# Spreading the running sums of a state-space scan over partitions by 32-row groups of ones

## The chip, the cores and the metric

One NeuronCore of a Trainium2 chip runs the whole kernel in one launch. The metric is the device time of an execution in microseconds (us). Two layers run in one loop on the chip, so each stage shows twice in a trace.

## The reference

The kernel is one inference step of a hybrid trunk: 128 context tokens and 256 latent tokens, width 1024, two layers. Each layer mixes tokens in three branches (latent attention, gated linear attention, and the state-space branch C), adds them through sigmoid gates, and then runs a mixture of experts. Only branch C is touched. Per head it does

```
acum   = cumsum(dt * A)                          # along the tokens of a chunk
Lm     = exp(acum[i] - acum[j])  for j <= i, else 0
y_diag = sum_j (C_i . B_j) * Lm[i, j] * dt_j * x_j
y_off  = (C_i . state) * exp(acum_i)
state  = exp(acum_last) * state + sum_j exp(acum_last - acum_j) dt_j x_j B_j
```

with 16 heads of 64 columns, two groups of B and C with 128 states each, and two directions. The matrix acum[i] - acum[j] is what the change is about: one factor of it, acum[i], has to lie along the free axis and be the same on all partitions j.

## The kernel before

Tokens come in three tiles of 128: tile 0 is the context, tiles 1 and 2 the latent tokens. The scan of branch C is one block of code with a stream of instructions for each engine (TensorE, VectorE, ScalarE, GpSimd, and SyncE for DMA), ordered by semaphores alone. It goes over six steps, `SCAN = ((0, 0), (1, 0), (0, 1), (1, 2), (0, 2), (1, 1))`, each a pair (direction d, tile t). The order within an engine is the order of the code.

TensorE, per step: `sc` (L1350), four matmuls of 16 columns that give the sums of 16 heads by token; `cb` (L1354), the products of B and C of two groups; `ai` (L1361), 16 matmuls, one for each head, of a column of `dta` broadcast to 128 by 128 as the stationary operand with the triangular matrix `rel(d)` as the moving one, four heads to a PSUM bank; `yo` (L1372, only t > 0), the old state times C; then a tile of the sigmoid gate of this branch, 16 records of L293, which has nothing to do with the scan and is put there as other work; `ds` (L1379, not in steps 4 and 5), what a step adds to the state; `yd` (L1387), 16 matmuls of 64 columns; and after tile 0 the transposes `so` (L325) of the state for the output. An fp32 matmul shows as two records in the trace.

VectorE, per step: `cb` times a mask (L1451); for each quarter q of the heads a subtraction from PSUM (L1457), a minimum with zero (L1461), and, one quarter late, a product with the masked `cb` (L1465); then the sums of y (L1472 and L1476 for `yo`, L1479 for `yd`), the state (L1486 for tile 0, else L1491 and L1493), and a one-column copy (L1496) that carries the semaphore `state_ready`. ScalarE copies and exponentiates `sc` into `ex2` (L1404, L1406) and exponentiates each quarter (L1410). GpSimd makes x times dt (L1436, L1439). Before the steps VectorE copies four transposed states (L1447).

The eight PSUM banks are handed out in turn: `claim` waits until the last user of the next bank was read, `makes` and `made` are the semaphore of a filled bank, `reads` and `read` that of a bank that was read. What stands behind a waiting claim on TensorE waits too.

After the scan TensorE runs the last two gate tiles (32 records of L293), while VectorE and ScalarE normalise y; the next block transposes y (L325).

Of the kernel before, what the change touches and what calls it, by code (L numbers as in the profile page):

```python
# [20 lines left out]
ALU = mybir.AluOpType  # L21
# [3 lines left out]
P = 128  # L25
# [62 lines left out]
GRP = 32  # L88
# [3 lines left out]
def trunk_kernel(nc, x, cond, consts, iota, vecs, rows, w_small, w_gate_low, router_w, cache_ckv, cache_krope,  # L92
                 state_gla, state_ssd, w_ada, w_in, a_wq, a_wkv, a_wo, b_wo, c_wo, w_out, e_w1, e_w3, e_w2,
                 y, new_ckv, new_krope, new_gla, new_ssd):
    with ExitStack() as ctx:
        def sb(name, shape):
            return ctx.enter_context(nc.sbuf_tensor(name, shape, F32))
# [15 lines left out]
        pick_row = sb("pick_row", [P, 2])  # L113
        mod = sb("mod", [P, 6, KD, 2])
# [14 lines left out]
            "xbc_ready", "ssd_state_in", "diff_ready", "decayed_ready", "mask_ready", "xw_ready",  # L129
# [21 lines left out]
        def counts(name):  # L151

            count[name] = count.get(name, 0) + 1
            return sem[name], 1
# [330 lines left out]
        with nc.Block() as block:  # L485
# [15 lines left out]
            @block.vector  # L501
            def _(dve):
                dve.memset(lowT[2 * RANK:2 * RANK + 1, :], 1.0).then_inc(*counts("dve_step"))
                dve.wait_ge(*counted("dve_step"))
                dve.memset(scond[:, :, :], 0.0).then_inc(*counts("cond_clear"))
                dve.wait_ge(*counted("cond_clear"))
                dve.wait_ge(sem["xin"], 64)
                ids = ident.rearrange("p (g r) -> p g r", r=GRP)
                dve.tensor_reduce(pick_row[:, 0:1], ids[:, :, 0], AX_X, ALU.add).then_inc(*counts("dve_step"))
                dve.tensor_reduce(pick_row[:, 1:2], ids[:, :, 1], AX_X, ALU.add).then_inc(*counts("dve_step"))  # L510
                dve.wait_ge(*counted("dve_step"))
                features_dve(dve, "x", xT)
# [55 lines left out]
        with nc.Fori(0, DEPTH) as l:  # L568
# [660 lines left out]

            gT_c = [carve(9728 + T * k, T) for k in range(3)] + [carve(3072 + T * k, T) for k in range(KD - 3)]  # L1230
# [106 lines left out]
            with nc.Block() as block:  # L1337
                @block.tensor
                def _(pe):
                    gate_pe(pe, W_GC, "gc", 0)  # L1340
                    pe.wait_ge(*following(pe, "ssd_state_in", 32))
                    for d in range(2):
                        for q in range(2):
                            transposed(pe, ("si", d, q), [ssd_in[:, d, 4 * q + i, :] for i in range(4)])
                    for s, (d, t) in enumerate(SCAN):
# [10 lines left out]
                        ins.then_inc(*makes(("cb", s)))  # L1356
                        for q in range(4):
                            out = claim(pe, ("ai", s, q))
                            for i in range(4):
                                h = H_C * d + 4 * q + i  # L1360
                                ins = pe.matmul(out[:, P * i:P * i + P], dta[:, t, h:h + 1].broadcast_to([P, P]), rel(d),  # L1361
                                                start=True, stop=True)
                            ins.then_inc(*makes(("ai", s, q)))
# [10 lines left out]
                        if s + 1 < len(SCAN):  # L1374
                            gate_pe(pe, W_GC, "gc", s + 1)
# [66 lines left out]
                def _(dve):  # L1442
                    dve.wait_ge(*following(dve, "yoff_ready"))
                    for d in range(2):
                        for q in range(2):
                            dve.wait_ge(*made(("si", d, q)))
                            dve.tensor_copy(ssd_s[:, d, 512 * q:512 * q + 512], bank(("si", d, q))).then_inc(*reads(("si", d, q)))  # L1447
                            dve.wait_ge(*read(("si", d, q)))
                    for s, (d, t) in enumerate(SCAN):
                        dve.wait_ge(*made(("cb", s)))  # L1450
# [3 lines left out]
                        for q in range(5):  # L1454
# [7 lines left out]
                            if q:  # L1462
# [4 lines left out]
                                dve.wait_ge(*counted("mask_ready"))  # L1467
                        for g in range(G_C):
# [698 lines left out]
```

## Time and profile before

| | us |
|---|---|
| median of 3 runs (2783.02 to 2785.2) | 2784.48 |
| profiled execution | 2785.75 |
| its span, first to last instruction | 2783.9 |
| TensorE busy | 2454.4 |
| VectorE busy | 893.8 |
| mean granted TensorE clock | 0.927 |
| scan of branch C in layer 1 (first `sc` to the last gate tiles) | 772.8 to 883.5 |
| same in layer 2 | from 2151.8 |

In the trace PE is TensorE's matmul, PEld its load of a stationary operand, DVE is VectorE, ACT ScalarE, POOL GpSimd, SP SyncE. L1361 is line 1361 of the kernel. PEclk is the granted share of TensorE's clock: 1.00 is 2.4 GHz, 0.50 is 1.2 GHz. A row of a timeline merges instructions of one kind that follow each other closely; behind its count, in brackets, is the idle time of the engine before it and what ended it. Busy times of matmuls are modelled ends, so the start of the next line is the better mark.

### The profile page before, as it was taken

What the parts mean: (1) busy time and instruction counts of PE and PEld (TensorE: products, weight loads), DVE (VectorE), ACT (ScalarE), POOL (GpSimd) and SP (SyncE); (2) the same over time, 40 slices, a digit from 0 to 9 for tenths busy, and PEclk for the clock granted to TensorE, in tenths of its full rate; (3) what the DMA queues carried; (4) which work ended last, traced back from release to release, by engine and by line L of the source; (5) the groups of instructions that cost most, each with busy time, mean ns of one, the idle gap of its engine ahead of it and who ended that gap; (6) DMA issues with size and microseconds to landing.
All of it is one profiled execution on the core that took longest, in us unless ns stands there. A gap on an engine that the chain in (4) does not pass through costs nothing. (4 is left out here: it accounts for less than half of the span.)

```text
span 2783.9 us, 39618 instructions
## 1 busy us (share of the span) xinstructions
PE 2454.4 (88%) x16902; PEld 1508.4 (54%) x16902; DVE 893.8 (32%) x1492; ACT 510.1 (18%) x906; POOL 106.0 (4%) x74
## 2 busy tenths in 40 slices
PE   6999999889899969999479999997898999599893
PEld 3546654554576545555245476555545765455552
DVE  2255312431558130000113562224315661300002
ACT  1133202210223021010021241022102220201000
POOL 0000000000021000000000000001001110000000
PEclk8999999899989979999789999898999899699996
DMA  6321132114314277999353201411243222799972
GB/s 241 106 93 61 54 140 93 46 61 151 125 32 146 91 297 272 376 373 345 115 184 112 93 31 62 165 61 46 71 159 117 89 78 91 298 346 379 375 272 80
DMA packets 162338, 440.60 MB, mean 158 GB/s; under 512 B 10150, under 2 KB 50086, under 8 KB 153448
## 3 DMA queue, kind: packets, MB, share of 16 engines
q1 hardware_dynamic: 144360, 412.75, 40.6%
q10 hardware_dynamic: 14336, 12.59, 1.5%
q0 software_dynamic: 3456, 12.58, 1.2%
q8 instruction: 140, 2.29, 0.3%
q14 instruction: 46, 0.38, 0.0%
HBM read 400.38 MB, written 37.52 MB: 157 GB/s over the span
## 5 line engine op out<-in xcount | busy, mean ns | idle before, releaser
L293 PE MATMUL ps<-space 128*128 128x384 f32 (+3 forms) x1696 | 475.5, 433 | 14.9 <-DVE space L469 8.5
L293 PE MATMUL ps<-hT,space 128*128 128x384 f32 x1344 | 461.3, 504 | 27.3 <-ACT hT L407 12.1
L293 PEld LDWEIGHTS ps<-space 128*128 128x128 f32 x1696 | 300.1, 194 | 187.7 <-issue 48.4
L293 PEld LDWEIGHTS ps<-hT,space 128*128 128x128 f32 x1344 | 262.0, 197 | 213.4 <-issue 41.4
L1673 PE MATMUL ps<-space 128*32 128x256 f32 x6144 | 343.7, 384 | 1.7 <-ACT space L1783 1.5
L293 PE MATMUL ps<-space,hT 128*128 128x512 f32 x768 | 336.7, 599 | 3.8 <-PEq L1191 3.8
L1673 PEld LDWEIGHTS ps<-space 128*32 128x32 f32 x6144 | 201.9, 111 | 133.8 <-issue 12.6
L293 PEld LDWEIGHTS ps<-space,hT 128*128 128x128 f32 x768 | 146.9, 192 | 192.0 <-issue 191.4
L1694 PE MATMUL ps<-space 128*32 128x256 f32 x3072 | 184.2, 398 | 1.5 <-DVE space L1915 1.5
L325 PE MATMUL ps<-cst,space 128*128 128x128 f32 x492 | 84.6, 324 | 90.5 <-DVE space L1927 29.8
L1694 PEld LDWEIGHTS ps<-space 128*32 128x32 f32 x3072 | 100.9, 115 | 74.2 <-issue 15.8
L325 PEld LDWEIGHTS ps<-cst,space 128*128 128x128 f32 x492 | 67.3, 167 | 119.7 <-DVE space L1927 32.4
L1910 DVE TENSOR_TENSOR space<-ps,space 128x384 f32<-128x384 f32 x32 | 17.8, 558 | 344.3 <-ACT space L1792 344.3
L381 DVE COPY space<-ps 128x512 f32<-128x512 f32 x24 | 16.6, 691 | 247.6 <-PE ps L366 247.5
L1656 PE MATMUL ps<-cst,space 96*128 96x96 f32 x256 | 31.8, 274 | 72.5 <-DMA space<-h_rows 72.3
L366 PE MATMUL ps<-space,scond 128*32 128x512 f32 x384 | 49.2, 637 | 42.6 <-issue 30.7
L293 PE MATMUL ps<-mT,space 128*128 128x384 f32 x256 | 83.1, 487 | 3.0 <-DVE space L1550 3.0
L1792 ACT ACTIVATE space<-ps 128x384 f32<-128x384 f32 x32 | 15.7, 490 | 331.3 <-PE ps L1673 331.3
L1915 DVE COPY space<-ps 128x384 f32<-128x384 f32 x32 | 17.8, 558 | 173.0 <-PE ps L325 173.0
L1656 PEld LDWEIGHTS ps<-cst,space 96*128 96x128 f32 x256 | 25.2, 154 | 86.4 <-DMA space<-h_rows 47.7
L293 PEld LDWEIGHTS ps<-mT,space 128*128 128x128 f32 x256 | 48.5, 190 | 37.6 <-DVE space L1550 4.2
L837 PE MATMUL ps<-space 96*128 96x384 f32 (+1 forms) x192 | 68.5, 442 | 0.1
(255 smaller groups left out, 2262.7 us busy)
## 6 DMA issues: line engine op xcount, KB each, us to landing
space<-in_e_w SPq DMA_DIRECT2D x96, 2048.0 KB, 15.2
space<-in_w_in SPq DMA_DIRECT2D x36, 2048.0 KB, 8.5
space<-in_w_ada SPq DMA_DIRECT2D x24, 2048.0 KB, 8.2
h_rows<-space SPq DMA_DIRECT2D x2, 6144.0 KB, 25.7
space<-h_rows SPq DMA_DIRECT2D x32, 384.0 KB, 17.9
y_rows<-mT ACTq DMA_DIRECT2D x128, 96.0 KB, 10.4
space<-in_a_wo SPq DMA_DIRECT2D x4, 2048.0 KB, 11.4
space<-in_b_wo SPq DMA_DIRECT2D x4, 2048.0 KB, 8.2
```

Of the source, the lines that this page charges most:

```text
L293: ins = pe.matmul(out, a, b, start=(i == 0), stop=(i == len(pairs) - 1))
L325: ins = pe.transpose(out[0:s.shape[1], i * P:i * P + P], s, ident)
L366: ins = pe.matmul(out[GRP * g:GRP * g + GRP, :], scond[:, k, :], w[:, k, :], start=(i == 0), stop=(i == KD // NGRP - 1))
L381: dve.tensor_copy(rows, bank(("mr", n))).then_inc(*reads(("mr", n)))
L837: pe.matmul(out[:, 0:P * (k1 - k0)], head_qT[0:QK, h % 2, tok(t)], head_kT[0:QK, h % 2, P * k0:P * k1], start=True, stop=True).then_inc(*m ...
L1656: ins = pe.transpose(out[:, SLOTS * i:SLOTS * i + SLOTS], tok_in[0:SLOTS, e % 2, P * k:P * k + P], ident[0:SLOTS, 0:SLOTS])
L1673: ins = pe.matmul(ps[TILE * c:TILE * c + TILE, B_UP + i // 2, 2 * P * (i % 2):2 * P * (i % 2) + 2 * P], hc[:, k, TILE * i:TILE * i + TILE] ...
L1694: ins = pe.matmul(ps[TILE * c:TILE * c + TILE, B_Y + i // 2, QD * (i % 2):QD * (i % 2) + QD], hidden[:, k, TILE * i:TILE * i + TILE], w2[: ...
L1792: act.activation(silc, up[:, :, up_first(e), :], ACT.Silu).then_inc(*counts("gated_ready"))
L1910: dve.tensor_tensor(gated, up[:, :, 1 - up_first(e), :], silc, ALU.mult).then_inc(*reads(("up", e)))
L1915: dve.tensor_copy(hidden.rearrange("p c (i s) -> p c i s", s=TILE), src).then_inc(*reads(("hid", e)))
```

## The change

The 16 matmuls of a step that broadcast one head each (L1361) go. In their place VectorE deals the 16 columns of `dta` into a matrix `dealt` of 128 columns that is zero elsewhere: head 4g + r goes to column 32g + r (`deal`). One matmul (`ar`) of this matrix with `rel(d)` gives the running sums of the 16 heads, head 4g + r on partition 32g + r. VectorE multiplies them by `pick_four`, a 128 by 4 matrix with ones where the partition is r modulo 32, into `block_rows`, 128 by 512, in which the partition 32g + r holds its head in columns 128r to 128r + 127 and zeros elsewhere (`blocks`), and a one-column copy carries the semaphore `block_ready`. Four matmuls then take 32 partitions each: ones (32 rows by 128 columns) as the stationary operand, 32 rows of `block_rows` with 512 columns as the moving one, each into a bank of its own, so that the sum over the 32 partitions spreads four heads over all 128 partitions, in the form that L1457 read before.

The deal and the block of a step are made in the step before it: `deal(s + 1)` at the start of step s, `ar` of s + 1 ahead of the gate tile, `blocks(s + 1)` behind the last product (L1465). Those of step 0 stand ahead of the steps, its block behind the four copies of L1447. The four banks of `ai` are now claimed one after the other before the first of the four matmuls, and `ar` takes one bank more in the round. `dealt` and `block_rows` lie in `wsm`, whose weights are used up by then.

```diff
--- before.py
+++ after.py
@@ -111,6 +111,7 @@
         condT = sb("condT", [P, KD, 2])
         scond = sb("scond", [P, KD, GRP])
         pick_row = sb("pick_row", [P, 2])
+        pick_four = sb("pick_four", [P, 4])
         mod = sb("mod", [P, 6, KD, 2])
         amp = sb("amp", [P, 2, KD, 2])
         dtraw = sb("dtraw", [P, NT, 32])
@@ -126,7 +127,7 @@
             "h_ready", "cqn_ready", "ckvn_ready", "sq_ready", "summed", "stat_ready", "head_root", "rotary_in",
             "nmax_ready", "abs_ready", "soft_ready", "logdecay_ready", "clamped_ready", "decay_ready",
             "qk_ready", "gla_state_in", "scaled_state", "state_ready", "o_ready", "conv_ready",
-            "xbc_ready", "ssd_state_in", "diff_ready", "decayed_ready", "mask_ready", "xw_ready",
+            "xbc_ready", "ssd_state_in", "diff_ready", "dealt_ready", "block_ready", "decayed_ready", "mask_ready", "xw_ready",
             "yoff_ready", "y_ready", "merged_ready", "chosen_ready", "zeros_ready", "zeroed", "rows_ready", "y_summed", "gated_ready", "y_scaled", "hidden_ready", "moe_ready", "stored",
             "act_step", "dve_step", "pool_step")
         sem = {n: ctx.enter_context(nc.semaphore(n)) for n in names}
@@ -508,6 +509,9 @@
                 ids = ident.rearrange("p (g r) -> p g r", r=GRP)
                 dve.tensor_reduce(pick_row[:, 0:1], ids[:, :, 0], AX_X, ALU.add).then_inc(*counts("dve_step"))
                 dve.tensor_reduce(pick_row[:, 1:2], ids[:, :, 1], AX_X, ALU.add).then_inc(*counts("dve_step"))
+                dve.wait_ge(*counted("dve_step"))
+                dve.tensor_reduce(pick_four[:, :], ident.rearrange("p (g r) -> p r g", r=GRP)[:, 0:4, :], AX_X, ALU.add
+                                  ).then_inc(*counts("dve_step"))
                 dve.wait_ge(*counted("dve_step"))
                 features_dve(dve, "x", xT)
 
@@ -1227,6 +1231,9 @@
             ssd_out = (carve(8192, KD, P), carve(25200, KD, P))
             ssd_tmp = carve(9216, 512)
 
+            w_flat = wsm[:, :, :].rearrange("p k n -> p (k n)")
+            block_rows = w_flat[:, 0:512]
+            dealt = w_flat[:, 512:768].rearrange("p (b n) -> p b n", b=2)
             gT_c = [carve(9728 + T * k, T) for k in range(3)] + [carve(3072 + T * k, T) for k in range(KD - 3)]
             mod_rows_c = carve(19344, 3, 512)
             zeros = carve(26256, QD)
@@ -1342,6 +1349,13 @@
                     for d in range(2):
                         for q in range(2):
                             transposed(pe, ("si", d, q), [ssd_in[:, d, 4 * q + i, :] for i in range(4)])
+
+                    def cumulative_rows(s):
+                        pe.wait_ge(*following(pe, "dealt_ready"))
+                        pe.matmul(claim(pe, ("ar", s))[:, 0:P], dealt[:, s % 2, :], rel(SCAN[s][0]), start=True, stop=True
+                                  ).then_inc(*makes(("ar", s)))
+
+                    cumulative_rows(0)
                     for s, (d, t) in enumerate(SCAN):
                         col = slice(OUT_COL[t], OUT_COL[t] + P)
                         a = dta[:, t, H_C * d:H_C * d + H_C]
@@ -1354,13 +1368,12 @@
                             ins = pe.matmul(out[:, P * g:P * g + P], xbc[:, 8 + g, col], xbc[:, 10 + g, col],
                                             start=True, stop=True)
                         ins.then_inc(*makes(("cb", s)))
+                        pe.wait_ge(*following(pe, "block_ready"))
                         for q in range(4):
-                            out = claim(pe, ("ai", s, q))
-                            for i in range(4):
-                                h = H_C * d + 4 * q + i
-                                ins = pe.matmul(out[:, P * i:P * i + P], dta[:, t, h:h + 1].broadcast_to([P, P]), rel(d),
-                                                start=True, stop=True)
-                            ins.then_inc(*makes(("ai", s, q)))
+                            claim(pe, ("ai", s, q))
+                        for q in range(4):
+                            pe.matmul(bank(("ai", s, q)), ones[GRP * q:GRP * q + GRP, :], block_rows[GRP * q:GRP * q + GRP, :],
+                                      start=True, stop=True).then_inc(*makes(("ai", s, q)))
                         if t:
                             for g in range(G_C):
                                 if s in FIRST:
@@ -1372,6 +1385,7 @@
                                 pe.matmul(claim(pe, ("yo", s, g)), xbc[:, 10 + g, col],
                                           ssd_s[:, d, 512 * g:512 * g + 512], start=True, stop=True).then_inc(*makes(("yo", s, g)))
                         if s + 1 < len(SCAN):
+                            cumulative_rows(s + 1)
                             gate_pe(pe, W_GC, "gc", s + 1)
                         pe.wait_ge(*following(pe, "xw_ready"))
                         if s not in LAST:
@@ -1440,13 +1454,34 @@
 
                 @block.vector
                 def _(dve):
+                    dve.memset(dealt, 0.0).then_inc(*counts("dve_step"))
+                    dve.wait_ge(*counted("dve_step"))
+                    dve.tensor_copy(dealt[:, 0, :].rearrange("p (g r) -> p g r", r=GRP)[:, :, 0:4],
+                                    dta[:, 0, 0:H_C].rearrange("p (g r) -> p g r", r=4)).then_inc(*counts("dealt_ready"))
                     dve.wait_ge(*following(dve, "yoff_ready"))
                     for d in range(2):
                         for q in range(2):
                             dve.wait_ge(*made(("si", d, q)))
                             dve.tensor_copy(ssd_s[:, d, 512 * q:512 * q + 512], bank(("si", d, q))).then_inc(*reads(("si", d, q)))
                             dve.wait_ge(*read(("si", d, q)))
+
+                    def deal(s):
+                        d, t = SCAN[s]
+                        out = dealt[:, s % 2, :].rearrange("p (g r) -> p g r", r=GRP)[:, :, 0:4]
+                        dve.tensor_copy(out, dta[:, t, H_C * d:H_C * d + H_C].rearrange("p (g r) -> p g r", r=4)
+                                        ).then_inc(*counts("dealt_ready"))
+
+                    def blocks(s):
+                        dve.wait_ge(*made(("ar", s)))
+                        dve.tensor_tensor(block_rows.rearrange("p (r n) -> p r n", r=4), each(bank(("ar", s))[:, 0:P], 4),
+                                          over(pick_four[:, :], P), ALU.mult).then_inc(*reads(("ar", s)))
+                        dve.wait_ge(*read(("ar", s)))
+                        dve.tensor_copy(stat_c[:, 0:1], cst[:, 0:1]).then_inc(*counts("block_ready"))
+
+                    blocks(0)
                     for s, (d, t) in enumerate(SCAN):
+                        if s + 1 < len(SCAN):
+                            deal(s + 1)
                         dve.wait_ge(*made(("cb", s)))
                         dve.tensor_tensor(cbm, quad(bank(("cb", s))[:, 0:G_C * P]), each(cum(d), G_C), ALU.mult).then_inc(*reads(("cb", s)))
                         dve.wait_ge(*read(("cb", s)))
@@ -1465,6 +1500,8 @@
                                 dve.tensor_tensor(decayed[:, 4 * r:4 * r + 4, :], quad(diff[:, r % 2, :]),
                                                   each(cbm[:, r // 2, :], 4), ALU.mult).then_inc(*counts("mask_ready"))
                                 dve.wait_ge(*counted("mask_ready"))
+                        if s + 1 < len(SCAN):
+                            blocks(s + 1)
                         for g in range(G_C):
                             out = y_c[:, t, 512 * g:512 * g + 512]
                             if t:
```

## Rows read from the trace of the kernel before

**Rows 1.** The page's table of engines: busy us, share of the span, instructions.
```profile
PE 2454.4 (88%) x16902; PEld 1508.4 (54%) x16902; DVE 893.8 (32%) x1492; ACT 510.1 (18%) x906; POOL 106.0 (4%) x74
```

**Rows 2.** Groups by line: engine, operation, tiles, shape, count | busy us, mean ns | idle before.
```profile
L1361 PE MATMUL ps<-cst,space 128*128 128x128 f32 x384 | 52.3, 300 | 0.3
...
L1457 DVE TENSOR_TENSOR space<-ps,space 128x512 f32<-128x512 f32 x48 | 33.1, 689 | 8.5 <-PE ps L1361 6.1 <-ACT space L1406 1.1
```

**Rows 3.** Stretches by step: us, busy of PE, PEld, DVE, ACT, POOL, PEclk, DMA share, GB/s.
```profile
772.80:792.40 19.60, 17.25 (x107) 14.06 (x106) 14.41 (x21) 5.97 (x9) 3.86 (x2) 0.92 0.00 1
792.40:815.40 23.00, 20.65 (x106) 17.46 (x106) 12.04 (x20) 5.97 (x9) 3.86 (x2) 0.80 0.00 0
815.40:834.60 19.20, 19.20 (x101) 15.17 (x101) 11.93 (x20) 5.97 (x9) 3.86 (x2) 0.88 0.20 65
834.60:852.00 17.40, 17.33 (x102) 13.10 (x102) 15.81 (x25) 5.97 (x9) 4.30 (x2) 1.00 1.06 368
852.00:867.70 15.70, 15.63 (x98) 12.37 (x98) 14.95 (x23) 5.97 (x9) 4.29 (x2) 1.00 0.37 119
867.70:883.50 15.80, 13.04 (x82) 11.76 (x82) 14.97 (x22) 4.20 (x7) 3.86 (x2) 0.83 0.00 1
```

**Rows 4.** Stretches at the lower clock: three of the first layer, one of the second.
```profile
789.40:799.50 10.10, 8.84 (x42) 8.87 (x43) 4.93 (x9) 2.31 (x4) 3.42 (x2) 0.50 0.01 2
813.30:820.00 6.70, 6.36 (x30) 6.39 (x31) 2.06 (x5) 1.68 (x3) 1.01 (x1) 0.50 0.01 2
878.10:888.30 10.20, 10.20 (x35) 8.08 (x35) 9.42 (x12) 2.93 (x5) 0.00 (x0) 0.50 0.01 2
...
2168.40:2178.50 10.10, 8.86 (x42) 8.89 (x43) 4.93 (x9) 2.31 (x4) 3.44 (x2) 0.50 0.01 2
```

**Rows 5.** Timeline, steps 0 and 1: start, length, engine, line, tiles, count [idle before, releaser].
```profile
771.80 2.87 DVE L1447 COPY space<-ps 128x512 f32<-128x512 f32 x4 [9.57 <-PE ps L325]
...
774.18 3.74 PE L1361 MATMUL ps<-cst,space 128*128 128x128 f32 x32
...
777.75 5.33 PE L293 MATMUL ps<-hT,space 128*128 128x384 f32 x16
...
782.91 1.88 PE L1379 MATMUL ps<-space 128*128 128x512 f32 x4
...
784.63 3.68 PE L1387 MATMUL ps<-space 128*128 128x64 f32 x32
...
786.63 0.69 DVE L1479 TENSOR_TENSOR space<-ps,space 128x512 f32<-128x512 f32 x1 [1.69 <-PE ps L1387]
...
790.66 1.94 PE L325 MATMUL ps<-cst,space 128*128 128x128 f32 x8 [2.35 <-DVE space L1486]
...
794.95 5.27 PE L1361 MATMUL ps<-cst,space 128*128 128x128 f32 x26
...
800.73 5.33 PE L293 MATMUL ps<-hT,space 128*128 128x384 f32 x16
```

**Rows 6.** Timeline, end of the scan.
```profile
877.36 6.41 PE L1387 MATMUL ps<-space 128*128 128x64 f32 x32 [2.76 <-issue]
...
883.56 12.90 PE L293 MATMUL ps<-hT,space 128*128 128x384 f32 x32
```

**Rows 7.** Timeline of TensorE: 32-column groups of L366 between full matmuls.
```profile
703.71 1.92 PE L366 MATMUL ps<-space,scond 128*32 128x512 f32 x16
705.56 10.91 PE L293 MATMUL ps<-hT,space 128*128 128x384 f32 x33
```

**Rows 8.** Timeline, start of step 3.
```profile
834.64 1.02 PE L1350 MATMUL ps<-space,cst 128*128 128x16 f32 x8
...
836.03 4.07 PE L1361 MATMUL ps<-cst,space 128*128 128x128 f32 x32
...
838.93 0.15 DVE L1496 COPY space<-cst 128x1 f32<-128x1 f32 x1
838.95 0.97 PEld L1361 LDWEIGHTS ps<-cst,space 128*128 128x128 f32 x8 [0.26 <-DVE space L1493]
```

## The prediction

> **What bounds the kernel now.** I read the busy table first. TensorE is busy for 88% of the span and VectorE for 32% [rows 1], so on average TensorE sets the time; but the change touches one stage, so that stage has to be read by itself. The groups by line say what leaves: the 384 head records of L1361 are 52.3 us of both layers [rows 2], 4.4 us a step for 12 steps. That is an upper bound of the gain, worth its face only where TensorE's end is what the step waits for. The stretches by step (first layer) show that this changes inside the stage: steps 0 to 2 last 19.6, 23.0 and 19.2 us with VectorE busy 14.4, 12.0 and 11.9; steps 3 to 5 last 17.4, 15.7 and 15.8 with VectorE busy 15.8, 15.0 and 15.0 [rows 3]. In the first three TensorE, partly at its lower clock, is the limit; in the last three the two engines are nearly level, with VectorE short of idle time.
>
> The same rows and the stretches by clock show the second thing: the granted clock is half (1.2 instead of 2.4 GHz) for some 10 us from 789.4, 6.8 us from 813.3 and 10 us from 878.1, and the second layer repeats the first of them [rows 4]. Each begins around a pause of TensorE: 2.35 us idle at 790.66 behind the 64-column matmuls of L1387 and ahead of the 16-column ones of L1350, and 2.76 us at 877.36 [rows 5, 6]. At half clock the 16 gate matmuls (5.33 us at full) take about twice that.
>
> **The matmuls removed and added.** Removed are 32 records of 128 columns a step. At full clock they run from 774.18 to the gate's start at 777.75, 3.6 us [rows 5]; in steps 1 and 2 they are stretched by the low clock. Added are 8 records with 32 rows and 512 columns a step (four matmuls, each with two records as every fp32 one here), and two of 128 columns (0.22) for the running sums. No row shows 32-row groups. Upper bound: one after another, as the 512-column records of L1379, 4 in 1.72 us (782.91 to 784.63 [rows 5]), so 3.4 us. Lower bound: side by side, as the 32-column groups of L366, whose 16 records of 512 columns take 1.85 us from the first start to the next line's [rows 7], so 0.9 us for 8. I take 0.9, the nearest row, being also a quarter of the array per matmul; each writes a bank of its own.
>
> Going into a group and out again costs something: L366's 16 records would be four times 0.43, 1.71 us, and 1.85 passed [rows 7], so 0.1 to 0.2 us a step. The Trainium skill, TensorEngine Tiling (Array Packing), section Key Properties, says that a change of tiling mode (not of the tile alone) drains TensorE. Were only a change of tile at issue the term would be zero; by the rule each of 12 steps pays twice, some 2 us in all, and the 1.85 us of L366 agrees with it.
>
> **Work added to VectorE.** A step gains the deal (a copy of 16 columns: between L1496's 0.15 and L1457's 0.69 us; I take 0.17, as it is small like the first), the block product (512 columns out of PSUM with a broadcast operand, the form of L1457, 0.69) and the marker copy (0.15), with 0.03 between them: 1.1 us [rows 2, 8]. Ahead of the scan a memset and a deal lie in VectorE's 9.57 us of idling before L1447 [rows 5]; the reduction for pick_four lies before the layers, below 0.2 us. In steps 0 to 2 the 1.1 us lies in idle time (1.69 us before the first L1479 of step 0; by the busy times 5.2 us of step 0, 11.0 of step 1 and 7.3 of step 2 [rows 3]). In steps 3 to 5 that cover is gone: there it costs up to its own length in each step that has it (3 and 4).
>
> **Two new waits.** (a) TensorE now waits for block_ready ahead of the four matmuls. In step 0 the product stands behind four copies that end at 774.67 [rows 5]: 774.67 + 0.9 + a semaphore's 0.06 is 775.65 against a start at 774.18. Then 0.95 of matmuls, 0.22 and 0.2 of switching put the gate at 777.0 instead of 777.75: only 0.7 us early. From step 1 on the block is made a step ahead. (b) All four banks are claimed before the first matmul. Banks go round by eight, and by my count of the claims the third and fourth ones of steps 3 and 4 are those that the state update of the step before still has to read. Before, 24 of the 32 head records of such a step ran ahead of it and only the last 8 waited (838.95, released by L1493 [rows 8]). Now all of them wait, and behind them in TensorE's queue the yo matmuls, the next sums, the gate, ds and yd. TensorE is left with sc and cb (834.64 to 836.03, 1.4 us) for the 4.3 us from there to that release: it idles 2.9 us where it idled 0.26.
>
> **The sum, one layer.** Steps 0 to 2, if the clock keeps its pattern: 0.7 in step 0; in step 1 the heads shrink from 5.8 us (794.95 to 800.73 [rows 5]) to 1.9 at half clock, but the gate, 4 us earlier, runs its first five matmuls at half, which leaves 2.1; step 2 the same way, until VectorE binds, 0.8: together -3.6. If the clock stays low as long as TensorE has this much less to do, the earlier gate is simply slower: 0. I take the middle, -1.8. Step 3: from release to release TensorE needs 0.95 + 0.2 + 1.72 (yo) + 0.22 + 5.2 (gate) + 1.72 (ds) + 1.8 (first half of yd) = 11.8, then VectorE 8 operations of 0.725 = 5.8: 17.6 against 17.4 now, +0.2 to +0.4. To this comes the clock. An idle time of 2.9 us, with L1387 before it and the few-column sc beside it, is longer than the one of 2.35 that ended in half clock in both layers [rows 4, 5]; so I expect one more slow stretch in step 3 and one in step 4. The shorter kind (6.8 us) takes 3.4 us, the longer 5.1: step 3 +3.7. Step 4, without ds: release to end of yd 0.95 + 0.2 + 1.72 + 0.22 + 5.2 + 3.6 = 11.9, 15.3 with 3.4 lost, against 11.4 now; some of it lies beside VectorE's own +1.6 (1.1 of work and 0.5 of waiting for the first group): between +1.6 at full clock and +3.9, taken +3.0. Step 5 has VectorE's work unchanged and a longer TensorE pause ahead of yd, and behind the scan 32 gate matmuls of 12.90 us that half clock already stretches [rows 6]: 0 to +3.4, taken +1.0. Sum: -1.8 + 3.7 + 3.0 + 1.0 = +5.9 a layer, +11.8 for two.
>
> The profiled execution took 2785.75 us (span 2783.9 and 1.85 around it), 1.3 above the median of the runs, 2784.48. With the sum it would be 2797.6; set against the median, **2796**.
>
> **Rivals.** Full clock in the wait (not slower): the idle time of steps 3 and 4 stays below what lowers the clock. For it: 2.76 and 2.35 are not far off, and in steps 3 and 4 of now the clock is 1.00 [rows 3]; against it, both shorter pauses did lower it. Then -3.6 + 0.3 + 1.6 = -1.7 a layer, -3.4 in all, 2781. It decides wherever the granted clock of the stretch from the end of step 2 to the end of step 4 is above 0.95.
>
> The pauses at the ends of steps 0 and 1 stop lowering the clock as well, since they fall earlier: 5.1 and 3.4 us are to be had there, less what VectorE then limits, some 1.5: -7 a layer, 2770. Against it, the pauses themselves (VectorE's copies and the transposes after them) are unchanged.
>
> The groups don't run side by side, so the change doesn't do what it says: 3.4 us instead of 0.9. Step 0 gets 1.8 slower instead of 0.7 faster, steps 1 and 2 gain nothing, steps 3 and 4 pay 2.5 more each behind their wait: 1.8 + 6.2 + 5.5 + 1 = 14.5 a layer, 2813. The Trainium skill, TensorE: Matmul & The Clock Gate, Part 3, has four 32-row matmuls of 512 columns at 3.07 times the speed of serial ones; by that figure 8 records would be an estimated 1.1 us and this rival falls. No run here shows it yet.
>
> **Chances.** Forecast 0.55 (own range 2788 to 2806), full clock 0.20, better clock in the first steps too 0.08, serial groups 0.12, slow stretches of the longer kind everywhere 0.05 (about 2808). The range 2779 to 2811 leaves out the third, part of the second and half of the serial case. A measurement here tells 0.2%, 5.6 us, from no change. Faster than 2778.9: 0.08 and a quarter of the second, 0.13. Within: the rest of the second and a sixth of the forecast, 0.24. Slower: 0.63.
>
> **What would show it.** In the changed profile: the four 512-column matmuls take about 0.9 us in all (groups side by side) or 3.4 (serial); in steps 3 and 4 they start only behind the state update (L1493 of now), with TensorE idle 2 to 3 us ahead of them; the granted clock of those steps is 0.7 to 0.9 instead of 1.00; VectorE's busy time rises by 12 times 1.0 us; step 0 shortens by less than 1 us. The prediction is wrong if steps 3 and 4 keep full clock, or if they last no longer than 17.4 and 15.7 us; and its reason is wrong if the time comes from VectorE's added work with TensorE waiting for block_ready.

## The result, and the profile after

The changed kernel takes 2791.36 us (median of ten runs, 2788.95 to 2796.91) against 2784.39 for the kernel before in ten runs on the same chip: ratio 1.0027, 95% interval 1.0017 to 1.0038, so 5 to 11 us slower. Forecast was 2796 in a range of 2779 to 2811, "slower" at 0.63. The profiled execution took 2791.44 us, with a span of 2789.6.

The page's table of engines for the changed kernel, the line of [rows 1]:

```profile
PE 2441.3 (88%) x16638; PEld 1474.6 (53%) x16638; DVE 906.9 (33%) x1531; ACT 510.6 (18%) x906; POOL 105.9 (4%) x74
```

TensorE has 13.1 us less to do, VectorE 13.1 us more, and the kernel is slower. What TensorE gave up is seen by line (columns as in [rows 2]; L1375 the row groups, L1476 the block product, L1471 the deal):

```profile
L1375 PE MATMUL ps<-wsm,cst 32*128 32x512 f32 x96 | 21.3, 970 | 13.5 <-DVE space L1530 11.4 <-DVE space L1479 2.1
...
L1476 DVE TENSOR_TENSOR wsm<-ps,pick_four 128x512 f32<-128x512 f32 x12 | 8.3, 691 | 0.4
...
L1471 DVE COPY wsm<-space 128x16 f32<-128x16 f32 x10 | 4.4, 441 | 0.3
```

(The mean of 970 ns of a group record counts records that run at the same time, so it isn't the time that one adds.) The two numbers that matter stand behind the second bar: TensorE idles 13.5 us ahead of this line, where it idled 0.3 ahead of the old one [rows 2], and 11.4 of them end with L1530, the state update that reads the claimed banks.

The stretches by step, first layer, columns as in [rows 3] (the numbers in brackets count records); then those of the lower clock, as in [rows 4]:

```profile
775.00:793.60 18.60, 15.18 (x84) 11.05 (x83) 14.74 (x26) 5.98 (x9) 3.86 (x2) 0.94 0.00 0
793.60:814.90 21.30, 18.95 (x85) 13.36 (x84) 14.23 (x23) 5.98 (x9) 3.80 (x2) 0.74 0.00 1
814.90:833.20 18.30, 18.30 (x79) 11.85 (x79) 13.57 (x23) 5.97 (x9) 3.80 (x2) 0.81 0.20 66
833.20:853.50 20.30, 17.45 (x81) 10.92 (x80) 15.91 (x28) 5.98 (x9) 4.30 (x2) 0.83 1.07 371
853.50:872.10 18.60, 15.76 (x76) 10.15 (x76) 15.81 (x28) 5.98 (x9) 4.29 (x2) 0.82 0.14 41
872.10:888.60 16.50, 11.43 (x59) 9.27 (x58) 14.11 (x20) 4.20 (x7) 3.86 (x2) 0.74 0.00 1
...
791.40:801.40 10.00, 9.51 (x34) 6.69 (x35) 5.21 (x8) 1.68 (x3) 3.80 (x2) 0.50 0.01 2
811.90:821.90 10.00, 8.76 (x31) 5.93 (x32) 5.17 (x8) 1.68 (x3) 3.34 (x2) 0.50 0.00 0
835.70:842.40 6.70, 4.78 (x12) 1.76 (x13) 5.57 (x11) 1.31 (x4) 4.30 (x2) 0.50 1.08 383
856.20:862.90 6.70, 5.01 (x12) 1.99 (x13) 5.54 (x11) 1.32 (x3) 4.29 (x2) 0.50 0.01 3
880.10:893.60 13.50, 11.85 (x40) 9.69 (x41) 11.74 (x16) 3.75 (x7) 0.00 (x0) 0.50 0.01 1
```

Steps 0 to 2 got shorter (18.6, 21.3, 18.3 against 19.6, 23.0, 19.2) and steps 3 and 4 longer (20.3, 18.6 against 17.4, 15.7). The granted clock of steps 3 and 4 was 1.00 [rows 3] and is 0.83 and 0.82: two low stretches of 6.83 us each are new (lengths from the profile's own record of the granted clock; the rows cut them to 6.70), and both begin while TensorE waits. The one at the end of the scan grew from 10.24 to 13.65. The timeline of TensorE shows that wait (start, length, line, tiles, count, idle before and its releaser), in step 0 and in steps 3 and 4:

```profile
777.59 1.14 PE L1375 MATMUL ps<-wsm,cst 32*128 32x512 f32 x8 [1.07 <-DVE space L1479]
778.66 0.49 PE L1355 MATMUL ps<-cst,wsm 128*128 128x128 f32 x2
...
833.22 1.02 PE L1364 MATMUL ps<-space,cst 128*128 128x16 f32 x8
834.09 0.69 PE L1368 MATMUL ps<-space 128*128 128x128 f32 x4
837.62 2.09 PE L1375 MATMUL ps<-wsm,cst 32*128 32x512 f32 x8 [2.85 <-DVE space L1530]
839.64 3.38 PE L1385 MATMUL ps<-space 128*128 128x512 f32 x4
...
857.88 2.09 PE L1375 MATMUL ps<-wsm,cst 32*128 32x512 f32 x8 [2.85 <-DVE space L1530]
```

sc and cb end, TensorE stands for 2.85 us where it stood for 0.26 [rows 8], and the groups and the matmuls behind them then run at 1.2 GHz: 8 group records take 2.02 us (837.62 to 839.64), against 1.07 in step 0 at 2.4 GHz.

From the scan's start (the first entry of its block on VectorE's queue, at 762.47 before and 764.42 after) to the first transposes of the next block, a layer now takes 138.32 us for 135.06. The two layers' +3.26 make 6.5 of the 7.0 between the medians. In the first layer it comes from these parts (us, by the starts of sc, which is L1350 before and L1364 after, and of the transposes; changes from unrounded times):

| part | before | after | change | predicted |
|---|---|---|---|---|
| start to step 0 (one pair of sums more) | 10.37 | 10.60 | +0.23 | 0 |
| step 0 | 19.55 | 18.61 | -0.94 | -0.7 |
| steps 0 to 2 | 61.80 | 58.20 | -3.60 | -1.8 (of -3.6 to 0) |
| step 3 | 17.42 | 20.26 | +2.85 | +3.7 |
| step 4 | 15.70 | 18.65 | +2.96 | +3.0 |
| step 5 and tail | 29.78 | 30.60 | +0.82 | +1.0 |

### The profile page after: what moved, and what is told of

Read it like the earlier page. It is cut to its first block and busy times, and to the rows that moved or that the text cites. A ratio compares the mean times of both kernels' runs of the same rounds, so it can differ in the third digit from the quotient of the medians.

```text
span 2789.6 us, 39167 instructions
## 1 busy us (share of the span) xinstructions
PE 2441.3 (88%) x16638; PEld 1474.6 (53%) x16638; DVE 906.9 (33%) x1531; ACT 510.6 (18%) x906; POOL 105.9 (4%) x74
## 5 line engine op out<-in xcount | busy, mean ns | idle before, releaser
L294 PE MATMUL ps<-hT,space 128*128 128x384 f32 x1344 | 466.9, 508 | 27.4 <-ACT hT L408 12.1
L1829 ACT ACTIVATE space<-ps 128x384 f32<-128x384 f32 x32 | 15.7, 492 | 329.9 <-PE ps L1710 329.9
## 6 DMA issues: line engine op xcount, KB each, us to landing
space<-in_a_wo SPq DMA_DIRECT2D x4, 2048.0 KB, 11.4
```

What stands on the lines that cost most here:

```text
L294: ins = pe.matmul(out, a, b, start=(i == 0), stop=(i == len(pairs) - 1))
L1829: act.activation(silc, up[:, :, up_first(e), :], ACT.Silu).then_inc(*counts("gated_ready"))
```

## Experiments

The theory: the four claims ahead of the first matmul turn the last-bank wait of steps 3 and 4 into a 2.85 us stop of TensorE, the clock falls in it, and that eats what the row groups give in steps 0 to 2. The rivals: VectorE's added 1.1 us a step is the price of steps 3 and 4 and the stop only shows it; or block_ready is the wait that costs. Stage times below are from the scan's start to the next transposes, one layer of the profiled execution (before 135.06, after 138.32); in every kernel here the second layer repeats them within 0.3 us. Ratios are to runs of the kernel before made beside each kernel (median 2783.56 for the first four kernels, 2783.75 for the last four). The rest of a total is less steady: between the two scans, in code that no kernel here changes, the profiled executions take from 1241.2 to 1248.0 us. So the stage carries the argument, and a total can differ from it by several us.

**Row groups only where they gain.** Steps 0 to 2 keep the new form, steps 3 to 5 the 16 head matmuls with their own claims; deal, block product and sums of those steps go.

```diff
+                        if s < 3:
                             pe.wait_ge(*following(pe, "block_ready"))
...
+                        else:
+                            for q in range(4):
+                                out = claim(pe, ("ai", s, q))
+                                for i in range(4):
+                                    ...
```

> The row groups in steps 0 to 2 alone, steps 3 to 5 with the 16 head matmuls and without the added VectorE work. Theory (wait and clock): steps 0 to 2 keep their gain of about 3.4 us a layer, steps 3 to 5 last 17.4, 15.7 and 15.8 us again at full clock: 6.7 us under the kernel before, near 2778. Rival (VectorE's added work is what costs in steps 3 and 4): the same, as that work is gone there too. Rival (the gain of steps 0 to 2 is a chance position of the slow-clock stretches): within 2 us of the kernel before.

Measured: 2778.41 us, ratio to before 0.9982 (0.9970 to 0.9995). Steps 2, 3 and 4 (columns as before):

```profile
813.20:831.30 18.10, 18.10 (x78) 11.65 (x77) 12.67 (x20) 5.97 (x9) 3.80 (x2) 0.80 0.21 68
831.30:848.70 17.40, 17.33 (x102) 13.10 (x102) 15.82 (x25) 5.97 (x9) 4.30 (x2) 1.00 1.06 369
848.70:864.40 15.70, 15.63 (x98) 12.36 (x98) 14.96 (x23) 5.97 (x9) 4.30 (x2) 1.00 0.36 117
```

Steps 3 and 4 are those of before to 0.1 us, and steps 0 to 2 keep their gain: the stage takes 131.49, 3.6 less than before. So all of the loss goes with the change in steps 3 to 5: 5.8 us in steps 3 and 4, and 0.8 in step 5 and the tail, which falls from 30.60 to 29.81 (29.78 before). Which part of the change there makes it, the next two tell.

**Useless matmuls in the wait.** The claims stay; between the second and the third, TensorE writes into the first claimed bank what the row group then overwrites.

```diff
                             claim(pe, ("ai", s, q))
+                            if s in (3, 4) and q == 1:
+                                for _ in range(12):
+                                    pe.matmul(bank(("ai", s, 0))[:, 0:P], ones, rel(d), start=True, stop=True)
```

> The changed kernel with 24 more records of 128 columns (2.7 us, their result overwritten) in the wait of steps 3 and 4, before the last two claims. Theory (wait and clock): the granted clock stays 1.00 in steps 3 and 4, which fall from 20.3 and 18.7 us to about 17.7 and 16.7; 4.5 us a layer, the whole near 2782.5 although TensorE does more. Rival (VectorE's added work): steps 3 and 4 stay as long, the whole stays at 2791.

Measured: 2782.68 us, ratio 0.9994 (0.9985 to 1.0002); stage 132.49. Steps 3 and 4:

```profile
832.10:850.00 17.90, 17.74 (x104) 12.79 (x104) 16.57 (x28) 5.97 (x9) 4.29 (x2) 1.00 1.06 367
850.00:866.20 16.20, 16.04 (x100) 12.04 (x100) 15.42 (x26) 5.97 (x9) 4.30 (x2) 1.00 0.32 102
```

And the wait of step 3 in TensorE's timeline:

```profile
833.50 2.84 PE L1376 MATMUL ps<-cst 128*128 128x128 f32 x24
836.50 1.14 PE L1378 MATMUL ps<-wsm,cst 32*128 32x512 f32 x8 [0.16 <-DVE space L1533]
```

The groups are released by the same update as before, no earlier, and still the steps shorten from 20.26 and 18.65 to 17.91 and 16.19: 2.35 and 2.46 us were the lower clock. What is left over the kernel before, 0.49 a step, has two possible sources that this kernel doesn't part: the later start of the groups, and VectorE's work with the sums. The two layers of the stage give 11.7 us and the medians 8.7; between the scans the profiled execution took 2.4 us more than that of the changed kernel (1246.9 for 1244.5).

**VectorE's work without the waits.** Deal, block product, marker and sums stay; TensorE uses the 16 head matmuls in all steps and doesn't wait for block_ready.

```diff
-                        pe.wait_ge(*following(pe, "block_ready"))
                         for q in range(4):
-                            claim(pe, ("ai", s, q))
...
+                            out = claim(pe, ("ai", s, q))
+                            for i in range(4):
+                                ...
```

> VectorE's added work and the running-sum matmul as in the changed kernel, but the 16 head matmuls of before for the four 32-row ones (and no wait for block_ready). Theory (wait and clock): steps 0 to 2 hide VectorE's work and pay 0.2 each for the extra matmul, steps 3 and 4 grow by up to 1.1 each at full clock: +3 a layer, 2790, without slow stretches in steps 3 and 4. Rival (VectorE's added work): steps 3 and 4 grow by the 5.8 us a layer that the changed kernel shows, 2797.

Measured: 2780.78 us, ratio 0.9995 (0.9986 to 1.0004). The expectation of 2790 was wrong. Steps 3 and 4:

```profile
831.60:849.20 17.60, 17.53 (x104) 13.31 (x104) 16.54 (x28) 5.97 (x9) 4.29 (x2) 1.00 1.07 374
849.20:865.20 16.00, 15.93 (x101) 12.66 (x100) 15.22 (x26) 5.97 (x9) 4.29 (x2) 1.00 0.34 107
```

17.63 and 15.92 by the starts of sc, 0.2 more than before in each, not up to 1.1, and 0.22 is what the two records of the sums take on TensorE (838.61 to 838.83). VectorE's work is nearly free. Where it goes, the timeline of VectorE and GpSimd in step 3 shows:

```profile
836.06 0.85 DVE L1472 COPY wsm<-space 128x16 f32<-128x16 f32 x1
...
838.00 1.15 DVE L1497 TENSOR_SCALAR space<-space 128x512 f32<-128x512 f32 x1
...
847.71 0.69 DVE L1517 TENSOR_TENSOR space<-ps,space 128x512 f32<-128x512 f32 x1 [0.24 <-PE ps L1402]
...
836.96 1.90 POOL L1454 TENSOR_TENSOR space<-space 128x1024 f32<-128x1024 f32 x1
```

and the same places in the kernel before:

```profile
840.30 1.90 DVE L1461 TENSOR_SCALAR space<-space 128x512 f32<-128x512 f32 x1
...
850.54 0.69 DVE L1479 TENSOR_TENSOR space<-ps,space 128x512 f32<-128x512 f32 x1 [0.81 <-PE ps L1387]
...
840.00 1.90 POOL L1439 TENSOR_TENSOR space<-space 128x1024 f32<-128x1024 f32 x1
```

The minimum runs beside GpSimd's second product and ends just behind it. In the kernel before it began 0.30 us into that product (840.30 and 840.00) and took 1.90 us; pushed back by the deal it begins 1.04 into it and takes 1.15. So the deal is paid for by a shorter minimum. The block product and the marker go into idle time: VectorE's wait for yd ahead of the first sum of it shrinks from 0.81 us to 0.24. In step 4 there is no such wait, and VectorE's last sum starts 0.8 us later (867.32 - 849.23, against 869.36 - 852.05), but step 5 and the tail take this up, with 29.75 us for 29.78. So this rival is refuted, by this run and by the one above. The total is no measure of the added work: steps 0 to 2 take 3.4 us a layer less than before, at a granted clock of 1.00, 0.92 and 0.91 where it was 0.92, 0.80 and 0.88 [rows 3], because the low stretches came later and were shorter (the last section has the numbers).

**A claim right ahead of each matmul.** The first two banks are free early; does it help to use them?

```diff
                         for q in range(4):
-                            claim(pe, ("ai", s, q))
-                        for q in range(4):
-                            pe.matmul(bank(("ai", s, q)), ...
+                            pe.matmul(claim(pe, ("ai", s, q)), ...
```

> The changed kernel, each bank claimed right ahead of its matmul, so that the first two groups of steps 3 and 4 run ahead of the state update. Theory (wait and clock): TensorE's pause there shrinks only from 2.85 to about 2.3 us, the clock still falls, the first two groups no longer delay VectorE: 2789 to 2791; if the pause is now too short for the clock to fall, 2783. Rival (VectorE's added work): 2791.

Measured: 2788.43 us, ratio 1.0018 (1.0009 to 1.0027); stage 136.40. Steps 3 and 4 last 19.48 and 18.98. The timeline of TensorE in step 3:

```profile
834.83 1.13 PE L1373 MATMUL ps<-wsm,cst 32*128 32x512 f32 x4
836.20 1.12 PE L1373 MATMUL ps<-wsm,cst 32*128 32x512 f32 x2 [0.24 <-DVE space L1528]
837.65 1.12 PE L1373 MATMUL ps<-wsm,cst 32*128 32x512 f32 x2 [0.33 <-DVE space L1528]
```

And two stretches there, the third group's and two microseconds behind the fourth:

```profile
836.20:837.40 1.20, 1.12 (x2) 0.29 (x2) 1.17 (x2) 0.00 (x0) 1.16 (x1) 1.00 1.06 379
...
839.00:841.00 2.00, 2.00 (x4) 0.72 (x3) 1.94 (x3) 0.01 (x1) 1.61 (x1) 0.55 1.08 386
```

The total came near the 2789 to 2791 expected, but not for the reason given: no pause of 2.3 us is left. The 2.85 us of idle time are now two waits of 0.24 and 0.33, for the state update ahead of the third and of the fourth group, as the prediction's count of the banks has it. But at full clock one group occupies TensorE for 1.12 us where four at once take 1.14, so the time is filled with groups one behind the other, and yo starts 5.35 us after sc instead of 6.42 (838.70 - 833.35; 839.64 - 833.22). And the clock falls still, right behind them (0.55): TensorE was idle there for no more than 0.33 us at a time, but ran only the 32-row groups, one or two at once. The theory's words have to be widened by that: it isn't the idle time by itself. The low stretch is 3.4 us long in step 3 and 6.8 in step 4. Step 3 gains 0.78 us and step 4 loses 0.33; of the stage's 1.92 us, 1.46 come in the tail (29.14 for 30.60), where the low stretch lasts 10.24 us instead of 13.65, so the total says little on the order of the claims.

**The pause that was there before.** If stops cost by their clock, those at the ends of steps 0 and 1 do so in the kernel before. Ten useless matmuls into the bank of the state's transposes, ahead of the wait at the end of each pass over one direction:

```diff
                         if t == 0:
+                            out = claim(pe, ("so", d, 0))
+                            for _ in range(10):
+                                pe.matmul(out[:, 0:P], ones, rel(d), start=True, stop=True)
```

> The kernel before with 20 records of 128 columns (2.2 us, overwritten) in TensorE's pause of 2.35 us at the ends of steps 0 and 1. Theory (the pauses lower the clock and steps 1 and 2 pay for it): clock 1.00 from step 0 to step 4, step 0 18.7 us (from 19.6), step 1 18.6 (23.0), step 2 17.2 to 17.8 (19.3): 7 us a layer, the whole near 2770. Rival (the clock falls for another reason, or steps 1 and 2 are held by something else): the whole stays at 2784.

Measured: 2769.17 us, ratio 0.9950 (0.9932 to 0.9968); steps 0 to 2:

```profile
775.40:794.10 18.70, 18.59 (x126) 15.36 (x125) 13.92 (x21) 5.97 (x9) 3.86 (x2) 1.00 0.00 1
794.10:812.90 18.80, 18.69 (x126) 15.45 (x125) 13.47 (x20) 5.97 (x9) 3.86 (x2) 1.00 0.01 1
812.90:829.90 17.00, 17.00 (x102) 12.97 (x101) 13.32 (x20) 5.97 (x9) 3.86 (x2) 1.00 0.22 71
```

Nothing of the change is in this kernel; work that is thrown away takes 0.8, 4.2 and 2.2 us from the three steps, and 14.6 from the kernel, where the first kernel of this section took 5.2.

**Row groups in steps 0 to 2, with that filling.** The first kernel of this section with the same ten matmuls.

> hybrid_012 with the same 20 records in the same two pauses. Theory: steps 0 to 2 last 17.8, 17.2 and 17.4 us; against before_fill the row groups are then worth 0.9 + 1.4 + 0.2 = 2.5 us a layer, less than the 3.4 they gave with the slow stretches, since at full clock VectorE holds step 2: near 2766. Rival (the 32-row groups are worth the same at any clock, 3.4 us a layer): near 2763.

Measured: 2769.88 us, ratio 0.9944 (0.9923 to 0.9964). Steps 0 to 3:

```profile
773.60:791.40 17.80, 16.63 (x104) 12.44 (x103) 14.36 (x26) 5.97 (x9) 3.87 (x2) 1.00 0.00 0
791.40:808.90 17.50, 16.84 (x105) 12.58 (x104) 14.42 (x23) 5.97 (x9) 3.86 (x2) 1.00 0.00 1
808.90:823.60 14.70, 14.70 (x78) 9.79 (x77) 12.98 (x19) 5.97 (x9) 3.87 (x2) 1.00 0.24 86
823.60:842.80 19.20, 17.47 (x102) 13.16 (x102) 16.11 (x26) 5.97 (x9) 4.13 (x2) 1.00 1.06 366
```

At full clock the groups are worth 2.7 us a layer of the stage (125.28 against 127.97 without them), near the 2.5 expected; but step 2 gains more than expected and step 3 gives 1.8 back, since VectorE isn't done when TensorE comes: the last head matmuls wait 1.73 us for the state update, of which one multiplication (L1543) takes 2.13 us beside GpSimd's products where such a one takes 0.69 alone. Between the totals the runs don't tell: 2769.88 and 2769.17 with overlapping intervals. That the groups are worth 5 us in this setting is shown for the stage, in both layers of one profiled execution, not for the total (2766 was expected, which lies inside the interval too).

**The block product of step 0 ahead of the state copies.** It stands behind four copies in VectorE's queue, and TensorE waits for it 1.07 us in step 0.

```diff
+                    cumulative_rows(0)
                     for d in range(2):
                         for q in range(2):
                             transposed(pe, ("si", d, q), ...
-                    cumulative_rows(0)
```

(with the same order on VectorE)

> The changed kernel with the first block made ahead of the four state copies and transposes. Theory (the wait for block_ready holds step 0): TensorE's first row groups start 1.1 us earlier, step 0 falls from 18.6 to about 17.5 us and the stage by as much, 2.2 us in all, 2789, if the slow stretches keep their place; a shifted stretch can add or take up to 3 us a layer. Rival (the wait for block_ready costs nothing): step 0 stays at 18.6 us.

Measured: 2791.95 us, ratio 1.0025 (1.0015 to 1.0035), no change from the 2791.36 of the changed kernel; step 0 takes 18.59 us, as the rival had it. Its timeline in step 0, TensorE, then GpSimd, then VectorE:

```profile
775.39 0.96 PE L1364 MATMUL ps<-space,cst 128*128 128x16 f32 x8
...
787.54 2.00 PE L1401 MATMUL ps<-space 128*128 128x64 f32 x16 [0.55 <-DVE space L1500]
...
778.24 1.90 POOL L1450 TENSOR_TENSOR space<-space 128x1024 f32<-128x1024 f32 x1 [7.56 <-ACT space L1420]
780.21 1.97 POOL L1453 TENSOR_TENSOR space<-space 128x1024 f32<-128x1024 f32 x1
...
778.97 1.45 DVE L1496 TENSOR_SCALAR space<-space 128x512 f32<-128x512 f32 x1
...
781.05 1.41 DVE L1496 TENSOR_SCALAR space<-space 128x512 f32<-128x512 f32 x1
```

TensorE no longer waits for block_ready, and VectorE starts its first subtraction (L1492) 2.86 us after sc instead of 3.83 (778.25 - 775.39; 778.85 - 775.02). But now two minima fall beside GpSimd's products instead of one, and the first takes 1.45 us where the changed kernel needs 0.47. VectorE's last product ends 12.1 us after sc in the kernel before, the changed kernel and this one alike, and the wait comes back as 0.55 us ahead of the second half of yd. The wait for block_ready in step 0 costs nothing.

**What they point to.** Row groups in steps 0 to 2, the filling, the early block, and the seventh gate tile moved from behind the scan into TensorE's pause of step 5 (useful work in place of filling).

```diff
                             gate_pe(pe, W_GC, "gc", s + 1)
+                        else:
+                            gate_pe(pe, W_GC, "gc", s + 1)
...
-                    for g in range(len(SCAN), KD):
+                    for g in range(len(SCAN) + 1, KD):
```

> hybrid_fill with the early first block and with the seventh gate tile moved from behind the scan into TensorE's pause of step 5. Theory: 1.1 us less in step 0; in step 5 the clock stays up and yd ends as before, and behind it one gate tile is left instead of two, so that VectorE's normalisation ends the stage some 3 us earlier: 4 us a layer under hybrid_fill, near 2758. Rival (the end of the stage is not held by the two gate tiles): only the 1.1 us, near 2764.

Measured: 2762.45 us, ratio 0.9919 (0.9900 to 0.9938), 21 us under the kernel before and 29 under the changed one. The interval (2756 to 2766) holds the 2758 expected and the 2764 of the rival, so the total doesn't choose; the trace does, part by part. The end of the scan in TensorE's timeline:

```profile
867.53 5.32 PE L294 MATMUL ps<-hT,space 128*128 128x384 f32 x16
872.69 3.68 PE L1413 MATMUL ps<-space 128*128 128x64 f32 x32
876.21 5.38 PE L294 MATMUL ps<-hT,space 128*128 128x384 f32 x16
```

No idle time is left ahead of yd (2.76 in [rows 6]), and the one gate tile behind it takes 5.38 us at full clock where two took 12.90. From the last sc to the transposes it is 26.37 us for 29.78, and the stage takes 121.77 in the first layer. Against the kernel with the filling (125.28) that is 3.4 us from the gate tile, near the 3 expected; the 1.1 us expected from the early block don't come, and step 0 stays at 17.81 (17.82).

## Why the prediction was right

The main mechanism was the one forecast: the row groups run side by side, the four claims stop TensorE in steps 3 and 4, and the clock falls in that stop. Two smaller parts, VectorE's work and the end of step 0, came out otherwise (below). Removed and added matmuls: groups side by side, 8 records in 1.07 us, near the 0.9 + 0.2 of the prediction; the rival of serial groups (3.4 us) is out. By the 3.07 times that the Trainium skill gives (TensorE: Matmul & The Clock Gate, Part 3) the estimate was 1.1 us, and the trace agrees with that time: 1.07. The ratio depends on what serial groups would take, which no kernel here runs at full clock without waits between them: by the 3.4 of the prediction it is 3.2, by one group alone (1.05 us from its start to that of yo, 837.65 to 838.70, in the kernel with a claim ahead of each) it would be 3.9. VectorE's busy time rose by 13.1 us for 12 times 1.1 worked out and 12 times 1.0 named as the mark, but that match is luck: by line the added operations take 18.2 us (8.3 for the block products, 4.4 for ten deals and 3.0 for the two ahead of the scan, 2.5 for the rest), and the minimum fell from 37.3 to 33.4. The four claims: 2.85 us of idle time for 2.9. The clock of steps 3 and 4: 0.83 and 0.82 in the 0.7 to 0.9 named. The rival of full clock in the wait (2781) is what the useless matmuls bring about, and they gave 2782.68.

Off were sizes, which made the forecast 5 us too high:

- **Steps 0 to 2, taken -1.8, measured -3.60 a layer: the mis-sized term.** The end that was not taken, the kept clock pattern (-3.6), is nearly the one that came: the low stretch around the end of step 0 lasts 10.24 us as before, and though the next one grew from 6.83 to 10.24, steps 1 and 2 gained 1.74 and 0.91 (2.1 and 0.8 were worked out). That the sum meets -3.6 so closely is partly luck, as the clock didn't keep its pattern. The middle between two ends was a value that neither mechanism gives. Both layers: 3.6 us too high.
- **Step 3, taken +3.7, measured +2.85.** The 3.4 us for a stretch of 6.83 at half clock took TensorE for busy throughout. In the 6.70 us row of step 3 it is busy for 4.78; half of that, 2.4, is what the clock can cost, and 2.35 is what filling gave back. While TensorE waited, the low clock cost nothing here.
- **Step 4, taken +3.0, measured +2.96,** but not as split: 2.46 is the clock and 0.49 the rest. Of the +1.6 for VectorE, the 1.1 for its work was wrong (0.2 at most by its own run). The prediction had the cover gone in steps 3 to 5; there was still an idle time of 0.81 us in step 3, a step 5 that takes up what step 4 leaves, and a minimum that stands beside GpSimd's product and gets shorter as it is pushed back.
- **Step 0 (wait for block_ready).** -0.94 for -0.7. The gate started 0.94 us earlier after sc, but the late block isn't what keeps the gain so small: with the block early and the gate another 1.1 us sooner, the step still takes 18.6. VectorE's last product, held up beside GpSimd, comes no sooner. Whether that alone sets the end isn't shown, as yd of the changed kernel runs through without a wait for it.
- **Step 5 and tail, taken +1.0, measured +0.82,** with the longer low stretch that was the reason given.

Open remains how the 0.49 us a step with filling divides between the later groups and VectorE, why the stop at the end of step 1 is followed by 10.24 us of low clock in the changed kernel and by 6.83 before, and what moves the time between the scans by up to 7 us from kernel to kernel.

## What to carry to other kernels

Row groups gained here only with all their output banks free at once (four took 1.07 us, one alone 1.05): before merging many small ones, look at who still reads the last bank, because the early matmuls were what TensorE did until then. Cost a new stop of TensorE by its clock as well: the length of the low stretch that it starts, times half of TensorE's busy share in it (2.4 us for 2.35 in step 3, 2.5 for 2.46 in step 4; for the two stretches of [rows 4] that the filling removed, 7.6 for 7.2); putting work into the stop, best some that has to be done anyway, gets this back without removing the wait. And read a change in busy time against what the engines do to one another: 1.1 us more on VectorE cost 0.2 or less.

## What the hardware showed

VectorE's minimum over 512 columns (L1496) lasts 0.43 us alone and up to 2.14 beside GpSimd's products:

```profile
L1496 DVE TENSOR_SCALAR space<-space x48: 426/427/2143, 779.6 to 2264.8; 128x512 f32<-128x512 f32 x48
```

(minimum, median and maximum in ns). In step 0 of the kernel with the early block, shown above, GpSimd's first product ends at 780.14 and the second at 782.18, and the two minima end, by the start of the next operation, at 780.34 and 782.38: 0.20 behind each, whenever they began. The deal, a copy of 16 columns, takes 0.17 us alone and 0.84 or 0.85 beside GpSimd in steps 3 and 4, where it ends with GpSimd's first product (836.06 + 0.85, against 834.49 + 2.39, in the kernel with VectorE's work alone), so its mean of 441 ns is not its size. The Trainium skill, SBUF — State Buffer, section SBUF: two separate sides, has VectorE and GpSimd share a pair of ports by an exclusive lock held for a whole instruction, not by splitting its bandwidth; ends that keep to GpSimd's, 0.20 us behind them for the minimum, agree with it.

Small shifts went with large changes of the clock. In the kernel with VectorE's work alone, TensorE's yd of step 0 ended 0.45 us later than in the kernel before; the fall of the clock came 30.3 us behind the scan's start instead of 26.9, and lasted 3.41 us instead of 10.24, in both layers. Why it was so much shorter isn't shown. In the totals such a stretch weighs as much as the whole change, so a total here says little without the stretches by clock beside it.
